# One body for the experts' second pass on TensorE, looped 32 times instead of two bodies looped 16 times

## The reference, cut to what matters

```python
def hier_moe(h, w_grp, b_grp, w_exp, b_exp, w_gate, w_up, w_down):
    ...
    gate = jax.nn.one_hot(grp, MOE_GROUPS, dtype=jnp.float32)[:, :, None] * (g_gate * within)[:, None, :]
    y = jnp.zeros((t.shape[0], d), jnp.float32)
    for gi in range(MOE_GROUPS):
        hid = jax.nn.silu(jnp.einsum('td,edf->tef', t, w_gate[gi])) * jnp.einsum('td,edf->tef', t, w_up[gi])
        hid = hid * gate[:, gi, :, None]
        y = y + jnp.einsum('tef,efd->td', hid, w_down[gi])
    return y.reshape(bsz, s, d).astype(h.dtype)
```

## Time and profile before

| | us |
| --- | --- |
| median of 3 runs | 988.38 (985.36 to 988.75) |
| span of the profiled execution, first to last instruction | 981.9 |
| TensorE busy in it | 947.7 |
| VectorE busy | 395.2 |
| ScalarE busy | 196.5 |

### The profile page before, as it was taken

One profiled execution on the slowest core, in us unless ns is written; L12 is line 12 of the kernel. 1 busy time (PEld: TensorE's weight loads), 2 busy tenths in 40 slices (PEclk: granted clock), 3 DMA queues, 4 the chain that ended last, 5 costly groups with the idle time before them and its releaser, 6 DMA issues.

```text
span 981.9 us, 12424 instructions
## 1 busy us (share of the span) xinstructions
PE 947.7 (97%) x4968; PEld 587.8 (60%) x4968; DVE 395.2 (40%) x860; ACT 196.5 (20%) x392; POOL 11.1 (1%) x21
## 2 busy tenths in 40 slices
PE   9999999999999999999999999999989999999985
PEld 5578558553333333388999999998575433333322
DVE  4324423341121212376666666756634312121205
ACT  3005402032122121212011110111122222222102
POOL 1110000000000000000000000000000000000000
PEclk9999999999999999999999999999998999999988
DMA  9894294459999999999767655753693699999992
GB/s 342 290 355 139 86 382 175 149 216 385 389 429 429 426 425 417 375 286 243 198 154 181 158 149 137 234 188 136 271 424 134 255 373 430 428 427 429 424 355 91
DMA packets 116279, 282.55 MB, mean 288 GB/s; under 512 B 4726, under 2 KB 82886, under 8 KB 104200
## 3 DMA queue, kind: packets, MB, share of 16 engines
q1 hardware_dynamic: 114784, 278.18, 76.9%
q0 software_dynamic: 1168, 3.40, 1.0%
q10 hardware_dynamic: 280, 0.31, 0.1%
HBM read 280.76 MB, written 1.11 MB: 287 GB/s over the span
## 4 chain that ended last, share of the span: by engine, by line
PE 88%; DMA 8%; DVE 2%; issue 1%; ACT 1%; SPq 0%; DVEq 0%
PE banks L1307 81%; DMA ring<-expert_w_up_in 7%; PE banks L1310 4%; PE banks L1702 2%; DMA ring<-xkv_w_in 1%; ACT late L852 0%; DVE scratch L2589 0%; ACT nrm L1052 0%; DVE mx L2298 0%; DVE nrm L2240 0%; DVE nrm L2306 0%; DVE scratch L2501 0%; DVE tmp L2092 0%; DVE late L845 0%; DVE late L2340 0%
## 5 line engine op out<-in xcount | busy, mean ns | idle before, releaser
L1307 PE MATMUL banks<-ring,scratch 128*64 128x512 f32 (+2 forms) x1696 | 424.8, 571 | 13.2 <-DMA ring<-expert_w_up_in 7.2
L1307 PEld LDWEIGHTS banks<-ring,scratch 128*64 128x64 f32 (+1 forms) x1696 | 160.3, 148 | 220.4 <-issue 219.6
L1307 PE MATMUL banks<-late,ring 128*128 128x256 f32 (+1 forms) x704 | 119.6, 330 | 0.8 <-ACT late L852 0.7
L1307 PEld LDWEIGHTS banks<-late,ring 128*128 128x128 f32 x704 | 107.4, 191 | 11.0 <-issue 1.6
L1007 ACT ACTIVATE scratch<-banks 128x512 f32<-128x512 f32 (+4 forms) x84 | 57.9, 701 | 279.8 <-PE banks L1310 193.5
L1307 PE MATMUL banks<-scratch 128*128 128x128 f32 (+5 forms) x492 | 110.5, 390 | 1.5 <-DVE scratch L2589 1.5
L2583 DVE TENSOR_SCALAR scratch<-banks 32x1024 f32<-32x1024 f32 x28 | 34.2, 1223 | 190.8 <-PE banks L1307 190.6
L1307 PEld LDWEIGHTS banks<-scratch 128*128 128x128 f32 (+2 forms) x492 | 60.8, 173 | 44.6 <-issue 38.5
L1307 PE MATMUL banks<-ring,late 128*128 128x512 f32 (+3 forms) x288 | 82.8, 442 | 1.0 <-DVE late L2340 1.0
L1307 PE MATMUL banks<-scratch,ring 128*128 128x128 f32 (+1 forms) x464 | 70.0, 308 | 0.7 <-DMA ring<-xkv_w_in 0.7
L1307 PEld LDWEIGHTS banks<-ring,late 128*128 128x128 f32 x288 | 49.2, 190 | 30.8 <-issue 24.9
(11 more groups left out here) (213 smaller groups left out, 677.9 us busy)
## 6 DMA issues: line engine op xcount, KB each, us to landing
ring<-expert_w_gate_in SPq DMA_DIRECT2D x22, 2048.0 KB, 15.4
ring<-expert_w_down_in SPq DMA_DIRECT2D x22, 2048.0 KB, 12.9
ring<-expert_w_up_in SPq DMA_DIRECT2D x20, 2048.0 KB, 16.4
ring<-odd_w_in_in SPq DMA_DIRECT2D x72, 512.0 KB, 6.5
ring<-expert_w_down_in SPq DMA_DIRECT2D x24, 512.0 KB, 8.5
ring<-xkv_w_in SPq DMA_DIRECT2D x4, 2048.0 KB, 11.9
scratch<-expert_w_gate_in SPq DMA_DIRECT2D x4, 2048.0 KB, 10.0
ring<-expert_w_up_in SPq DMA_DIRECT2D x16, 512.0 KB, 8.0
```

Source lines behind the costliest of these rows:

```text
L1307: return giving_back(nc.tensor.matmul(dst, lhsT, rhs, start=start, stop=stop))
```

## The change

Three things change in the second pass, for both layers. TensorE's body is written once and its loop runs 32 times (`Fori(0, TILES * EXPERTS)`). Since one body must serve both tiles, it reads the tile's rows from a fixed place (`rest_rows`, in `third_slot`), where ScalarE copies them before each tile. The other three engines go tile by tile, outside the loop over the experts, so that each has two loops of 16 turns with half the former body. One semaphore is added for each layer (`rows`). `kcur` and `gcur` shrink from two columns to one, so that `key`, `gates` and `column` lie two words lower in `scratch`. The flag, its test and everything outside the bodies are the same.

```diff
-        kcur = a.take(TILES)
-        gcur = a.take(TILES)
+        kcur = a.take(1)
+        gcur = a.take(1)
...
+        rest_rows = third_slot[:, 0:D].rearrange("p (c q) -> p c q", c=CH)
...
                 with sp.If(flag > 0):
                     sp.wait_ge(gate_ps, l * DUOS + DUOS // 2 + 1)
-                    with sp.Fori(0, EXPERTS) as e:
-                        for k in range(2):
-                            sp.wait_ge(s["sel"], e * 2 + k + 1)
+                    for k in range(TILES):
+                        with sp.Fori(0, EXPERTS) as e:
+                            sp.wait_ge(s["sel"], e + (k * EXPERTS + 1))
...
                 with act.If(flag > 0):
                     act.wait_ge(hid_sb, (l + 1) * DUOS - 1)
-                    with act.Fori(0, EXPERTS) as e:
-                        for k in range(2):
-                            act.wait_ge(s["gate_ps"], e * 2 + k + 1)
+                    for k in range(TILES):
+                        if k:
+                            act.wait_ge(s["parts"], k * EXPERTS)
+                        copy(rest_rows.rearrange("p c q -> p (c q)"), rows(k)).then_inc(s["rows"], 1)
+                        with act.Fori(0, EXPERTS) as e:
+                            act.wait_ge(s["gate_ps"], e + (k * EXPERTS + 1))
...
                     pe.wait_ge(hT_sb, (l + 1) * DUOS - 2)
-                    with pe.Fori(0, EXPERTS) as e:
-                        for k in range(2):
-                            pe.wait_ge(s["sel"], e * 2 + k + 1)
-                            flip(bank[0][:, 0:P], gselr)
-                            for c in range(CH):
-                                last = mm(bank[2 + c // 4][:, (c % 4) * P:(c % 4 + 1) * P], nrm[:, k, c, :], selr, True, True)
+                    with pe.Fori(0, TILES * EXPERTS) as i:
+                        pe.wait_ge(s["sel"], i + 1)
+                        flip(bank[0][:, 0:P], gselr)
+                        for c in range(CH):
+                            last = mm(bank[2 + c // 4][:, (c % 4) * P:(c % 4 + 1) * P], rest_rows[:, c, :], selr, True, True)
...
                 with dve.If(flag > 0):
                     piece_in(dve, f"selT{l}{GROUPS - 1}")
-                    with dve.Fori(0, EXPERTS) as e:
-                        for k in range(2):
+                    for k in range(TILES):
+                        dve.wait_ge(s["rows"], k + 1)
+                        with dve.Fori(0, EXPERTS) as e:
```

## The result

| | before | changed |
| --- | --- | --- |
| median of 4 runs, us | 988.06 (985.36 to 988.75) | 976.11 (975.08 to 979.22) |
| ratio of the runs, 95% interval | | 0.9907 (0.988 to 0.9933) |
| span of the profiled execution, us | 981.9 | 974.6 |
| that execution's own time, us | not listed | 976.23 |

The changed kernel is faster by 0.7 to 1.2%, 6.6 to 11.9 us. The spans differ by 7.3 us, and the forecast for the span was 974.5.

The account below looks back on a forecast made before the run. TensorE, busy 97% of the span, was taken to bound the kernel; layer 1's jump gains 7.4 us and the other terms are about zero, so 988.4 - 7.4 = 981.0 us, range 977.5 to 984.0.

Parts of the forecast that it names:

- The code does not run: Both layers branch over the second-pass bodies, so no executed instruction is added or removed; 4968 load and multiply pairs.
- TensorE's jump in layer 1: Branch over the second-pass body, 6.177 us before, stops missing its instruction packet and takes 0.455 us: gain 7.44 us.
- The 0.26 us: Stall and slow clock make 7.70 us, the difference between layers 7.44; the rest was taken as made up later.
- The reading of the distances: TensorE's test to target: a jump into the next 256-instruction packet is cheap, past it a miss; layer 1's reached 562, over 512.
- TensorE's jump in layer 0: Branch over layer 0's second-pass body: target in the same packet or the next, held either way; zero.
- the loop: Loop over the heads, 1082 instructions: held whole in instruction memory, so shifting it by 149 costs zero.
- the other engines: ScalarE's, VectorE's and SP's jumps over the bodies: tests stay at 0.05 to 0.07 us; zero to 0.5 us.
- What takes the stall's place: Last down matrices' loads in layer 1 are issued earlier too: costs 0 to 0.05 us, up to 0.5 if transfers come late.
- From the span to the time: Median of the runs lies 6.5 us over the profiled span, carried over unchanged: 988.4 - 7.4 = 981.0 us.
- Nothing changes: Rival, 7%: layer 1's 5.11 us is not the jump's distance but a slow fetch or profiler effect; 988.4 us.
- Half comes back: Rival, 5%: layer 1's stall goes, but the clock still falls over the 16 products there; 983.3 us.
- The loop's back edges: Rival, 3%: new alignment makes the back edge of the loop over the heads miss twice, +8.0 us net; 996 us.

Follow-up runs that it names:

- the padded changed kernel: Changed kernel plus 74 never-executed transposes (148 instructions) ending TensorE's second-pass body in both layers, jump 303 instructions: 984.55 us, ratio 1.000 to the kernel before.
- the last runs: Kernel before with 15, 20, 24 or 28 never-executed transposes added to layer 0's TensorE body: 985.36, 983.9, 978.0 and 979.0 us.
- 48 instructions of padding: Kernel before with 24 never-executed transposes added to layer 0's TensorE second-pass body: 978.0 us in one run.
- the later comparison: Changed kernel unchanged, run again beside the kernel before on the same chip: 976.77 us (6 runs) against 984.94 (24 runs), ratio 0.9923.
- the kernels with 85 and 150 transposes: Kernel before with never-executed transposes in TensorE's second-pass body: 85 in layer 0, 985.53 us, ratio 0.9995; 150 in both layers, 991.92 us, ratio 1.0059.
- 40 instructions of padding: Kernel before with 20 never-executed transposes added to layer 0's TensorE second-pass body: 983.9 us in one run.

## Why the prediction was right, and where it was off

**The code does not run.** Right: 4968 pairs after as before, and the counts of TensorE, VectorE, ScalarE and GpSimd on the page are the same.

**TensorE's jump in layer 1.** Right in cause and size. I took 7.44 us from the two layers as twins; the spans differ by 7.3 us, and the padded changed kernel brings back 7.67 us of stall and slow clock. The 0.26 us that I took to be made up later was not: layer 1's stretch from the transposes to the output copy went from 36.20 to 28.49 us, 7.71 us less, which is the full 7.70 of stall and slow clock. The twins themselves differ by 28.76 - 28.49 = 0.27 us.

The reading of the distances held in kind: the jump of 304 passed over a packet, the one of 155 does not. My count of layer 1's test, 258 instructions behind its packet's call, was too high. By the edge that the last runs give it stands 40 to 48 instructions ahead of a packet's end, at 208 to 216, and 208 + 304 is 512, so the jump missed by at most some 8 instructions. That is why 48 instructions of padding are enough. The term that was mis-sized is the sequencer's lead over the engine: I subtracted 30 from the 288 instructions of the earlier trace rows, and 288 less 208 to 216 is 72 to 80, if the call comes at the packet's edge. The changed kernel's target, which I put at 264, in the next packet, then lies at 214 to 222, in the test's own; held either way. The queue moved 32 packets, not the 33 that I forecast by dividing the program's length by 256.

One step of the reading is not shown: that the sequencer calls the next packet on entering one. With 48 instructions of padding the test stands at most 8 behind the edge, some 1 us at the engine's pace, and still the packet was there 4.9 us ahead of the branch. Either the sequencer stood for a long time between edge and test, or the call has another cause. The gain doesn't hang on it.

**TensorE's jump in layer 0, the loop, the other engines.** Right at zero. The padded changed kernel shows it for the other engines together with the scratch addresses, to within 2 us. Both back edges of the loop are taken without a new packet: from 507 to 651 us none comes in the changed kernel's trace.

**What takes the stall's place.** Right: the SP issues moved with TensorE, and the last chunk's wait is not in the chain.

**From the span to the time.** This step failed. I carried over 6.5 us between the profiled execution's span and the median, and got 981.0; the median is 976.11, below the 977.5 that I gave as lower end. The profiled execution after has 976.23 - 974.6 = 1.6 us around its span, and in the later comparison the 24 runs of the kernel before have 1.9 us each (1.86 to 2.03). So about 4.6 of the 6.5 us were no time outside the span: the profiled execution, some 983.8 us long, was a quick one, and the three runs were slow ones. The 24 runs have a median of 984.94 (981.93 to 990.41), 3 us lower than the first 988, and the time goes with the clock: the mean granted clock was 0.988 in the run of 981.93 us and 0.979 in that of 990.41. Against that the changed kernel's 976.77 is 8.2 us lower by medians, and 7.6 by the ratio. I should have set the forecast as a difference and taken the absolute time as uncertain by the spread between executions, some 8 us.

**The rivals.** Nothing changes: out, by the interval 0.9893 to 0.9953, and the padded kernel shows that the distance was the cause; a full memory bus alone doesn't make the stall, since the transfers' share over the 16 products is 1.02 in the changed kernel too, with a quick branch. That a jump of 304 instructions would stay inside what TensorE holds, and cost nothing: out going forward, by the same jump at 6 us and at 0.44. Half comes back: out, the clock stayed at 1.00. The loop's back edges: 0.22 to 0.25 us in every trace, although the loop was shifted by up to 300 instructions.

## What to carry to other kernels

A branch over code that never runs took 6 us here, 5 of them idle, and left a slow clock behind it, and whether it did hung on at most 8 instructions of alignment; so when an edit of cold code moves the time, look at the duration of each engine's compare-and-branch and at the instruction queue before looking for a cause in the work. A jump well under one packet of 256 instructions (a float32 multiplication is four of them, as this program is built) can't pass over a whole packet, wherever it stands, and looping instead of writing out is a way to get one; with 155 instructions it was quick in both places seen, and no run tries a short jump at the most unlucky place. Twin stages of the same code in one trace are a good ruler for such a stall, here to 0.3 us.

## What the runs showed that I had not expected

- The price of one miss depends on the clock that follows it. Idle time and slow products together come to 6.7 and 6.8 us in layer 0 (the kernels with 85 and 150 transposes) and to 7.2 to 7.9 us in layer 1 (five traces), with the idle time itself 4.9 to 5.1 us each time.
- The quick branch has two levels. It took 0.23 to 0.24 us in the changed kernel, whose targets by my count lie in the test's own packet, and 0.34 to 0.47 us in the kernels whose targets lie in the next one. I read this as the cost of changing packets; no run tests it apart, and the loop's back edges speak against it: they go back over four packets in 0.22 to 0.25 us.
- The edge is sharp: 40 instructions of padding give 5.99 us, 48 give 0.43.
